# Sparse attention in a Trainium2 transformer kernel: value projections moved behind the queries, softmax factors one step later, values of an older pair before the turning of a younger one

## The chip, the cores and the metric

The kernel runs on one core of one Trainium2 chip. The metric is the device time of one execution in microseconds (us), lower is better.

## The reference

Two transformer blocks over 256 tokens of width 1024, in float32. The change touches one part of the second block, a sparse attention with three branches (compressed blocks, selected blocks, window) of 16 query heads in 4 groups:

```
kv = h @ w_kv                    # k_raw v_raw k_sel v_sel k_win v_win, 4 groups x 64
k_cmp, v_cmp = silu(blocks(k_raw) @ w1) @ w2, silu(blocks(v_raw) @ w1) @ w2
qg = h2 @ w_qg                   # 1024 query columns, 48 gate columns
gates = sigmoid(qg[..., 1024:])
p_c = softmax(q @ k_cmp.T + bias) * has_any
p_s = softmax(q @ k_sel.T + bias); p_w = softmax(q @ k_win.T + bias)
o = g0 * (p_c @ v_cmp) + g1 * (p_s @ v_sel) + g2 * (p_w @ v_win)
x = x + o @ w_o
```

With 256 tokens all selected blocks are taken, so the selected and the window branch see the same causal keys. `blocks` makes 15 overlapping blocks of 32 tokens.

## The kernel before

All is written by hand, engine by engine, each with its own in-order list of instructions; semaphores are waited for with `wait_ge`. SyncE loads the weights in chunks of 128 x 2048 into a ring of three slots (`raw`). For each chunk ScalarE writes a rounded high half (L385, `w_hi`), VectorE the rest (L724, `w_lo`, "a split"), and TensorE makes three products per tile of weights (high x high, high x low, low x high: L1362 to L1364, and L1425 to L1427 where tokens come out on partitions). Only when TensorE is through with chunk c (`chunk_used`) may the halves of chunk c + 3 be written: `nxt(c)` in ScalarE's and VectorE's lists.

Around the change the order is, before:

- TensorE: `kv_raw` 0 and 1, `k_att` 0 and 1, two transposes of the norm factor, `v_att` 0 and 1, query 0, the gates (48 products with 48 columns, L1425 to L1427), the first matrix of the compression (`phi`, four chunks, 96 products, L1782 to L1784), scores of pair 0 (L1711), query 1, query 2, small products of the compression, scores of pair 1, query 3, scores of the compressed branch (L1821, 32 records with 14 or 30 columns).
- VectorE: scaled raw values (L1175), 16 additions that lay out the blocks (L1185), splits, the low parts of the operand (L763), keys (L1194), values (L1201), low parts of the blocks (L741), query (L1210), gates, then the pair work.

Then a loop over eight pairs of heads. Step t issues, on TensorE, the scores of pair t (`n_score`), the turning (transposes) of the probabilities of pair t - 2 (`n_turn`, L1734 to L1739, banks 5 to 7), and the values of pair t - 3 (`n_out`, L1755 to L1763). On VectorE: `n_tops` adds the bias and takes the maximum of four parts per head in one custom instruction each (L1251), then a small instruction negates the maxima (L1254); `n_copies` copies turned probabilities out of PSUM (L1271, L1273); `n_factors` (L1262, L1264) waits for all eight exponentials of its pair. On ScalarE: `n_exps` (eight exponentials with sums, L673) and copies (L682, L684). On GpSimd two passes per pair multiply the probabilities by the factors (L288). In step 2 VectorE also does the softmax of the compressed branch (L1327 to L1334), in step 3 TensorE transposes it, and it is copied (L703, L1337). Scores of the next pair need the maxima of the last one, since the banks 2 to 4 are the only ones for scores.

Of the kernel before, what the change touches and what calls it, by code (L numbers as in the profile page):

```python
# [22 lines left out]
P = 128  # L23
# [23 lines left out]
          ("kv_raw", 2), ("k_att", 2), ("v_att", 2), ("nsa_q0", 1), ("nsa_gate", 1), ("phi", 4), ("nsa_q", 3),  # L47
# [8 lines left out]
NSA_Q_BANK = (6, 7, 6, 0)  # L56
PHI_BANK = (5, 0)
# [79 lines left out]
def program(nc, x_t, p_t, positions, weights, small, consts, rel_bias, bias_rows, bias_skew, out):  # L137
    with ExitStack() as ctx:
# [16 lines left out]
        nsa_p = nc.alloc_sbuf_tensor_at("nsa_p", [P, 4, S], F32, offset=x_at + 2 * 2 * 768 * 4)  # L155
        over = nc.sbuf_base
        gate_or_bias = sb("gate_or_bias", [P, 16, S])
        heads = sb("heads", [P, 16, S])
        x_f, y_f = sb("x_f", [P, KT, S]), sb("y_f", [P, KT, S])
        y_hl = sb("y_hl", [P, KT, 2, S], F32R)  # L160
# [4 lines left out]
        y_h, y_l = y_hl[:, :, 0, :], y_hl[:, :, 1, :]  # L165
        sq = sb("sq", [P, KT, S])
# [52 lines left out]
        n_near, n_ptx = sem("n_near"), sem("n_ptx")  # L219
# [10 lines left out]
        def cst(name, n, i=0):  # L230
# [29 lines left out]
        n_own = [flat(t_ab), nsa_p[:, 0:2, :].rearrange("p a b -> p (a b)"),  # L260
                 nsa_p[:, 2:4, :].rearrange("p a b -> p (a b)")]
# [56 lines left out]
        def _(pool):  # L318
# [49 lines left out]

            pool.wait_ge(op_lo, PC["blk_v"] + 1)
# [9 lines left out]
        def _(act):  # L379
# [269 lines left out]
            act.wait_ge(g_raw, 1)  # L649
            nc.scalar.activation(nsa_g[:, :, :], nsa_g[:, :, :], ACT.Sigmoid).then_inc(g_sig, 1)  # L650
            nxt(C["nsa_gate"])
            nxt(C["phi"])

# [13 lines left out]
            def n_exps(k):  # L667
# [3 lines left out]
                for m, ap in enumerate(n_parts(k)):  # L671
                    q, e, b = 1 - m // 2, k % 2, m % 2
                    nc.scalar.activation(ap, ap, ACT.Exp, bias=ns[:, 1, q, e, b:b + 1],  # L673
                                         accum_out=ns[:, 2, q, e, b:b + 1]).then_inc(n_exp, 1)
# [42 lines left out]
        def _(dve):  # L717
# [452 lines left out]
            for w in range(2):  # L1170

                dve.wait_ge(chunk_used, C["kv_raw"] + w + 1)
                if w == 1:
                    dve.wait_ge(blk_ready, 4)
# [833 lines left out]
```

## Time and profile before

| | |
|---|---|
| time of three runs, median (lowest to highest) | 1287.74 us (1286.16 to 1290.9) |
| the profiled execution: time, span | 1289.02 us, 1287.0 us |
| mean granted TensorE clock | 0.976 of 2.4 GHz |
| busy: TensorE, VectorE, ScalarE, GpSimd | 1233.5, 892.9, 647.1, 231.2 us |
| chain that ended last | TensorE 86%, VectorE 8%, ScalarE 4%, issue 2% |
| the sparse attention up to its output projection | 909.0 to 1073.3 us |

Times in the rows are microseconds from the start of the span. A row's bracket says how long the engine had been idle before it and what ended that. "PEclk" is the granted TensorE clock as a share of 2.4 GHz.

### The profile page before, as it was taken

The numbers are of one execution on the slowest core, as the hardware profiler recorded it, in microseconds if no ns is written. First come the engines' busy times: TensorE is split into PE (matmuls) and PEld (weight loads), VectorE is DVE, ScalarE is ACT, GpSimd is POOL, SyncE is SP. The second block draws the span as 40 slices with busy tenths as digits, with TensorE's granted clock in tenths as the row PEclk, the third lists the DMA queues.
The fourth block names the chain that finished last, engine by engine and source line by source line (L and its number), as shares of the span: only waits on it lengthen the run. The fifth ranks groups of instructions, "written<-read, shape, count | busy, mean of one in ns | idle before, by whom it ended". The sixth has DMA issues, their size and how long they took to land.

```text
span 1287.0 us, 19911 instructions
## 1 busy us (share of the span) xinstructions
PE 1233.5 (96%) x7952; PEld 1094.7 (85%) x7952; DVE 892.9 (69%) x1241; ACT 647.1 (50%) x851; POOL 231.2 (18%) x114
## 2 busy tenths in 40 slices
PE   5999999999999999999999999999999579999996
PEld 4888889977789888888999988888999448888885
DVE  6877667786867787766887776655767574766554
ACT  6655545541664665545633655444535454555441
POOL 1444200002000244400000045300001230355000
PEclk9999999998999999999999999999989799999998
DMA  6655554461635465555445455555555011455540
GB/s 260 212 183 192 197 196 171 157 229 32 166 107 173 159 218 182 189 194 197 164 164 196 166 205 189 194 197 194 199 197 197 33 34 66 166 194 197 196 164 33
DMA packets 31042, 217.35 MB, mean 169 GB/s; under 512 B 3408, under 2 KB 3584, under 8 KB 5488
## 3 DMA queue, kind: packets, MB, share of 16 engines
q1 hardware_dynamic: 29616, 210.66, 46.4%
q0 software_dynamic: 1344, 5.53, 1.7%
q8 instruction: 60, 0.98, 0.3%
q14 instruction: 22, 0.18, 0.0%
HBM read 215.10 MB, written 4.22 MB: 170 GB/s over the span
## 4 chain that ended last, share of the span: by engine, by line
PE 86%; DVE 8%; ACT 4%; issue 2%; DMA 0%; DVEq 0%; SPq 0%; ACTq 0%
PE bank L1369 37%; PE bank L1370 18%; PE bank L1362 7%; PE bank L1364 7%; PE bank L1363 7%; DVE w_hl L724 2%; ACT w_hl L385 1%; PE bank L1425 1%; PE bank L1426 1%; PE bank L1427 1%; DVE y_f L1185 1%; ACT x_f L673 1%; PE bank L1552 1%; PE bank L1711 1%; PE bank L1821 1%
## 5 line engine op out<-in xcount | busy, mean ns | idle before, releaser
L724 DVE TENSOR_TENSOR w_hl<-raw,w_hl 128x2048 fp32r<-128x2048 f32 x197 | 452.0, 2296 | 121.6 <-ACT w_hl L385 120.7
L385 ACT ACTIVATE w_hl<-raw 128x2048 fp32r<-128x2048 f32 x197 | 375.1, 1907 | 133.6 <-PE bank L1364 60.3
L1369 PE MATMUL bank<-x_hl,w_hl 128*128 128x512 f32 x864 | 303.1, 397 | 12.6 <-DVE w_hl L899 12.6
L1369 PE MATMUL bank<-hidden,w_hl 128*128 128x512 f32 x864 | 299.7, 394 | 0.0
L335 POOL TENSOR_TENSOR hidden<-hid_f,hidden 128x256 fp32r<-128x256 f32 (+1 forms) x76 | 189.4, 2492 | 529.1 <-ACT hidden L472 309.6
L1370 PE MATMUL bank<-x_hl,w_hl 128*128 128x256 f32 x864 | 240.6, 278 | 0.0
L1370 PE MATMUL bank<-hidden,w_hl 128*128 128x256 f32 x864 | 239.3, 277 | 0.0
L1369 PEld LDWEIGHTS bank<-x_hl,w_hl 128*128 128x128 f32 x864 | 163.3, 189 | 50.6 <-issue 12.5
L1369 PEld LDWEIGHTS bank<-hidden,w_hl 128*128 128x128 f32 x864 | 162.0, 188 | 37.6
L1362 PE MATMUL bank<-x_hl,w_hl 128*128 128x256 f32 x576 | 166.8, 290 | 1.0 <-DVE x_hl L741 0.6
L1363 PE MATMUL bank<-x_hl,w_hl 128*128 128x256 f32 x576 | 164.7, 286 | 0.0
L1364 PE MATMUL bank<-x_hl,w_hl 128*128 128x256 f32 x576 | 164.7, 286 | 0.0
L1370 PEld LDWEIGHTS bank<-x_hl,w_hl 128*128 128x128 f32 x864 | 163.5, 189 | 0.1
L1370 PEld LDWEIGHTS bank<-hidden,w_hl 128*128 128x128 f32 x864 | 162.2, 188 | 0.0
L451 ACT ACTIVATE second<-bank 128x512 f32<-128x512 f32 (+1 forms) x108 | 57.6, 533 | 199.2 <-PE bank L1370 199.2
L1369 PE MATMUL bank<-y_hl,w_hl 128*128 128x512 f32 x352 | 122.4, 394 | 0.0
L1362 PEld LDWEIGHTS bank<-x_hl,w_hl 128*128 128x128 f32 x576 | 112.2, 195 | 4.9 <-issue 2.6
L1363 PEld LDWEIGHTS bank<-x_hl,w_hl 128*128 128x128 f32 x576 | 112.4, 195 | 0.1
L1364 PEld LDWEIGHTS bank<-x_hl,w_hl 128*128 128x128 f32 x576 | 112.3, 195 | 0.0
L816 DVE TENSOR_TENSOR t_ab<-bank,second 128x512 f32<-128x512 f32 x76 | 52.6, 691 | 76.8 <-ACT second L451 58.6
L1362 PE MATMUL bank<-y_hl,w_hl 128*128 128x256 f32 (+1 forms) x352 | 100.3, 285 | 0.6 <-DVE w_hl L724 0.6
L1363 PE MATMUL bank<-y_hl,w_hl 128*128 128x256 f32 (+1 forms) x352 | 99.5, 283 | 0.0
(305 smaller groups left out, 1650.3 us busy)
## 6 DMA issues: line engine op xcount, KB each, us to landing
raw<-weights SPq DMA_DIRECT2D x198, 1024.0 KB, 4.9
bias_skew<-bias_rows POOLq DMA_DIRECT2D x1, 3072.0 KB, 23.6
gate_or_bias<-bias_skew POOLq DMA_DIRECT2D x1, 2048.0 KB, 10.7
h<-x_t SPq DMA_DIRECT2D x1, 1024.0 KB, 4.9
out_t<-x_f SPq DMA_DIRECT2D x4, 256.0 KB, 2.1
con<-consts SPq DMA_DIRECT2D x1, 672.5 KB, 12.2
heads<-p_t POOLq DMA_DIRECT2D x1, 256.0 KB, 3.1
par<-small SPq DMA_DIRECT2D x1, 199.5 KB, 4.9
```

Source lines behind the costliest of these rows:

```text
L335: nc.gpsimd.tensor_tensor(hidden[:, at, 1, :], src, hidden[:, at, 0, :].bitcast(F32), ALU.subtract).then_inc(hid_lo, 1)
L385: nc.scalar.activation(w_hi[:, s, :], raw[:, s, :], ACT.Copy).then_inc(hi_split, 1)
L451: nc.scalar.activation(dst, src, ACT.Copy).then_inc(second_out, 1)
L673: nc.scalar.activation(ap, ap, ACT.Exp, bias=ns[:, 1, q, e, b:b + 1], accum_out=ns[:, 2, q, e, b:b + 1]).then_inc(n_exp, 1)
L724: V.tensor_tensor(w_lo[:, s, :], raw[:, s, :], w_hi[:, s, :].bitcast(F32), ALU.subtract).then_inc(lo_split, 1)
L816: V.tensor_tensor(t_ab[:, :, :], bank[:, s:s + 2, 0:S], second[:, j % 2, :, :], ALU.add).then_inc(ab_ready, 1)
L1185: ins = V.tensor_tensor(dst[:, :, 2 * t + e, :], src[:, :, t, half:half + NCMP], pe[rows, :].rearrange("p (l n) -> p l n", n=1).to_broadca ...
L1362: mm(out_, w_hi[:, s, c:c + m], x[:, 0, :], start=start, stop=False, **kw)
L1363: mm(out_, w_hi[:, s, c:c + m], x[:, 1, :], start=False, stop=False, **kw)
L1364: return mm(out_, w_lo[:, s, c:c + m], x[:, 0, :], start=False, stop=stop, **kw)
L1369: mm(out_, w_hi[:, s, c:c + m], x, start=start, stop=False, **kw)
L1370: return mm(out_[:, 0:S], w_lo[:, s, c:c + m], x[:, 0, :], start=False, stop=stop, **kw)
```

## The change

The value projections leave their place behind the keys: chunk order, and order on all engines, put them behind the queries, one before the scores of the compressed branch and one behind scores 1. ScalarE evicts them (`v_in`) instead of VectorE. The gates are computed with features on partitions (24 products of 256 columns, weights padded to 128 columns) and turned by two transposes. The block layout goes to tiles of its own (`blk_h`, `blk_l`), with the second half of it behind the keys. Queries 1 to 3 come before any score. The softmax of the compressed branch stands before the loop, its transposes in step 2. `n_tops` gives the negated sum and its minimum, so that the negation goes; `n_exps` uses scale -1. In the loop VectorE makes the factors of pair t - 1 behind the maxima of pair t, and TensorE does the values of pair t - 3 ahead of the turning of pair t - 2.

```diff
-          ("kv_raw", 2), ("k_att", 2), ("v_att", 2), ("nsa_q0", 1), ("nsa_gate", 1), ("phi", 4), ("nsa_q", 3),
+          ("kv_raw", 2), ("k_att", 2), ("nsa_q0", 1), ("nsa_gate", 1), ("phi", 4), ("nsa_q", 3), ("v_att", 2),
...
-NSA_Q_BANK = (6, 7, 6, 0)
-PHI_BANK = (5, 0)
+NSA_Q_BANK = (3, 6, 7, 5)
+PHI_BANK = (1, 4)
...
# ScalarE
-            for j in range(1, 6):
-                nxt(c + j)
-            hi(x_hf[:, 0:960], y_flat[:, 0:960], blk_ready, 4, C["nsa_q0"])
-            hi(x_hf[:, 960:1920], y_flat[:, 960:1920], blk_ready, 8)
+            nxt(c + 1)
+            for j in range(2):
+                nxt(C["k_att"] + j)
+            hi(blk_h[:, 0, 0:960], y_flat[:, 0:960], blk_ready, 4)
             nxt(C["nsa_q0"])
...
+            hi(blk_h[:, 1, 0:960], y_flat[:, 960:1920], blk_ready, 8)
             nxt(C["nsa_gate"])
             nxt(C["phi"])
+            act.wait_ge(g_tr, 1)
+            nc.scalar.activation(nsa_g[:, :, :], bank[:, 5, 0:96].rearrange("p (a b) -> p a b", a=2),
+                                 ACT.Sigmoid).then_inc(g_sig, 1)
...
+            def v_in(w):
+
+                act.wait_ge(chunk_used, C["v_att"] + w + 1)
+                for t in range(2):
+                    nc.scalar.activation((n_vs, n_vw)[w][:, t, :], bank[:, 6 + w, t * 256:t * 256 + 256], ACT.Copy,
+                                         scale=r_tok[:, 0, t:t + 1]).then_inc(v_done, 1)
+
+            for j in range(1, 4):
+                nxt(NSA_Q[j])
             n_exps(0)
             n_exps(1)
-            nxt(NSA_Q[1])
-            n_exps(2)
-            n_exps(3)
-            nxt(NSA_Q[2])
+            v_in(0)
             for q in range(2):
                 c = c_p[:, q, :, :, 0:c_n[q]]
                 act.wait_ge(c_sub, q + 1)
                 nc.scalar.activation(c, c, ACT.Exp).then_inc(c_exp, 1)
+            n_exps(2)
+            n_exps(3)
+            nxt(C["v_att"])
+            v_in(1)
...
-                if t == 3:
+                if t == 2:
                     act.wait_ge(c_pt, 1)
                     nc.scalar.activation(c_t[:, 512:1024], bank[:, 1, :], ACT.Copy).then_inc(c_ptc, 1)
-                    nxt(NSA_Q[3])
+                if t == 4:
+                    nxt(C["v_att"] + 1)
...
# VectorE
+            for w in range(2):
+                raw_in(w)
                 nxt(C["kv_raw"] + w)
                 for j in range(2 * w, 2 * w + 2):
                     operand_piece("mix1", y_h, y_l, j)
             for w in range(2):
+                keys_in(w)
                 nxt(C["k_att"] + w)
+                blocks(0, (w,))
             dve.wait_ge(rt_mm, 2)
             st.done(V.tensor_copy(r_tok[:, 0, :], bank[:, SUMS, 0:256:128]))
...
+            lo(blk_l[:, 0, 0:960], y_flat[:, 0:960], blk_h[:, 0, 0:960])
+            blocks(1, (0, 1))
...
+            V.tensor_tensor(t_a[0:48, :], bank[0:48, 2, 0:S], r_sb[0:48, :], ALU.mult).then_inc(g_raw, 1)
             nxt(C["nsa_gate"])
+            lo(blk_l[:, 1, 0:960], y_flat[:, 960:1920], blk_h[:, 1, 0:960])
+            nxt(C["phi"])
...
-                    st.inc(V.tensor_tensor_reduce(dst, src, bias if m < 2 else bias[:, 128:256], 1.0, -3e38,
-                                                  ALU.add, ALU.max, ns[:, 0, 1 - m // 2, e, m % 2:m % 2 + 1]))
-                st.wait()
-                V.tensor_scalar(ns[:, 1, :, e, :], ns[:, 0, :, e, :], -1.0, None, ALU.mult).then_inc(n_max, 1)
+                    ins = V.tensor_tensor_reduce(dst, src, bias if m < 2 else bias[:, 128:256], -1.0, 3e38,
+                                                 ALU.add, ALU.min, ns[:, 1, 1 - m // 2, e, m % 2:m % 2 + 1])
+                ins.then_inc(n_max, 1)
...
             for t in range(2, PAIRS + 2):
                 if t < PAIRS:
                     n_tops(2 * t)
                     n_tops(2 * t + 1)
+                if t - 1 < PAIRS:
+                    n_factors(t - 1)
                 n_copies(t - 2)
-                if t < PAIRS:
-                    n_factors(t)
...
+                if t == 4:
+                    nxt(C["v_att"] + 1)
...
# TensorE
             query(0)
-            pe.wait_ge(kv_done, 5)
-            arrived(C["nsa_gate"] + 1)
-            tokens(C["nsa_gate"] % RING, lambda t: bank[:, 7, t * 48:t * 48 + 48], 48, range(KT), y_hl, 0,
-                   True, True).then_inc(chunk_used, 1)
...
+            c = C["nsa_gate"]
+            arrived(c + 1)
+            for k in range(KT):
+                last = product(bank[:, 2, 0:S], c % RING, k * P, P, y_hl[:, k, :, :], k == 0, k == KT - 1)
+            last.then_inc(chunk_used, 1)
...
+                if w == 0:
+                    pe.wait_ge(g_raw, 1)
+                    for t in range(2):
+                        ins = T(bank[:, 5, 48 * t:48 * t + 48], t_a[0:48, P * t:P * t + P],
+                                con[0:48, CN["ident"]:CN["ident"] + 48])
+                    ins.then_inc(g_tr, 1)
             query(1)
...
-            n_score(1)
+            pe.wait_ge(g_sig, 1)
             query(3)
-
+            pe.wait_ge(q_done, 1)
+            n_score(0)
...
+            pe.wait_ge(q_done, 3)
+            value(0)
             pe.wait_ge(q_done, 4)
             pe.wait_ge(cmp_done, 2)
...
             ins.then_inc(c_scores, 1)
+            n_score(1)
+            value(1)
 
             for t in range(2, PAIRS + 3):
                 if t < PAIRS:
                     n_score(t)
+                if t == 3:
+                    pe.wait_ge(c_ptc, 2)
+                if t >= 3:
+                    n_out(t - 3)
+                if t == 2:
+                    pe.wait_ge(v_done, 4)
                 if t - 2 < PAIRS:
                     n_turn(t - 2)
-                if t == 3:
+                if t == 2:
...
-                    pe.wait_ge(c_ptc, 2)
-                if t >= 3:
-                    n_out(t - 3)
```

## Rows read from the trace of the kernel before

**Rows 1.** Busy time by stretch: us, each engine busy (instructions), PEclk, DMA share, GB/s

```profile
909.00:1073.30 164.30, 140.09 (x1059) 122.40 (x1057) 108.62 (x266) 79.33 (x183) 27.35 (x18) 0.88 0.35 122
909.00:932.80 23.80, 23.80 (x198) 23.54 (x196) 19.86 (x33) 14.00 (x19) 1.20 (x1) 1.00 0.63 222
932.80:975.70 42.90, 40.41 (x289) 40.24 (x289) 29.74 (x30) 18.68 (x13) 0.95 (x1) 0.84 0.56 195
975.70:1009.70 34.00, 29.21 (x238) 27.64 (x237) 18.17 (x55) 14.42 (x37) 7.83 (x4) 0.87 0.44 157
1009.70:1073.30 63.60, 46.67 (x338) 30.98 (x337) 40.85 (x150) 32.23 (x115) 17.37 (x12) 0.85 0.05 18
```

**Rows 2.** Waits, 909 to 1073.3: who waited for whom, total, times, longest

```profile
PE bank L1755 <- DVE y_f L1337: 5.8, 1, 5.8
...
PE bank L1821 <- DVE heads L1210: 4.8, 1, 4.8
PE bank L1734 <- ACT nsa_t L684: 4.7, 3, 1.8
...
PE bank L1425 <- DVE w_hl L724: 2.5, 1, 2.5
```

**Rows 3.** Busy time by stretch: four at the lower clock, one not

```profile
936.40:939.80 3.40, 3.40 (x19) 3.40 (x18) 3.40 (x5) 0.00 (x0) 0.00 (x0) 0.52 0.88 306
956.80:966.90 10.10, 10.10 (x49) 10.10 (x49) 4.41 (x4) 2.88 (x3) 0.00 (x0) 0.50 0.35 117
1002.70:1014.70 12.00, 11.97 (x54) 10.90 (x55) 4.17 (x20) 1.31 (x5) 2.35 (x2) 0.50 0.26 87
1028.80:1035.10 6.30, 6.28 (x30) 3.65 (x32) 3.24 (x1) 1.21 (x1) 2.33 (x2) 0.50 0.15 25
...
1035.50:1062.30 26.80, 19.33 (x166) 12.76 (x164) 20.01 (x85) 16.30 (x64) 8.68 (x6) 1.00 0.08 32
```

**Rows 4.** Groups by line and shape, 909 to 1073.3: busy us, mean ns

```profile
L724 DVE TENSOR_TENSOR w_hl<-raw,w_hl 128x2048 fp32r<-128x2048 f32 x16 | 38.0, 2372 | 15.0 <-ACT w_hl L385 14.9
L385 ACT ACTIVATE w_hl<-raw 128x2048 fp32r<-128x2048 f32 x16 | 30.5, 1908 | 24.5 <-PE bank L1427 12.1 <-PE bank L1364 9.1 <-PE bank L1784 3.2
...
L1185 DVE TENSOR_TENSOR y_f<-t_ab,par 64x240 f32<-64x240 f32 x16 | 8.8, 572 | 0.3
...
L1271 DVE COPY nsa_t<-bank 128x512 f32<-128x512 f32 x8 | 5.5, 690 | 3.5 <-PE bank L1739 3.5
...
L763 DVE SCALAR_TENSOR_TENSOR y_hl<-h,par,y_hl 128x256 fp32r<-128x256 f32 x8 | 3.3, 479 | 0.0
```

**Rows 5.** The chain that ended last: start, us, what

```profile
1002.73 7.03 PE bank L1821 x32
```

**Rows 6.** Busy time by stretch: one step's scores, turning, values

```profile
1045.92:1047.42 1.50, 1.50 (x12) 1.08 (x13) 1.15 (x2) 1.50 (x8) 0.00 (x0) 1.00 0.00 0
1047.42:1048.92 1.50, 1.50 (x16) 1.33 (x14) 0.19 (x1) 1.50 (x8) 0.00 (x0) 1.00 0.05 11
1048.92:1051.13 2.21, 2.21 (x21) 1.05 (x20) 2.06 (x12) 0.26 (x1) 1.92 (x2) 1.00 0.00 0
```

**Rows 7.** Instructions in order of time, one step of the pair loop

```profile
1042.64 1.90 POOL L288 TENSOR_TENSOR x_f<-x_f,stat 128x1024 f32<-128x1024 f32 x1
1042.76 1.81 DVE L1254 TENSOR_SCALAR stat<-stat 128x4 f32<-128x4 f32 x1
...
1044.60 0.51 ACT L673 ACTIVATE second<-second,stat 128x256 f32<-128x256 f32 x1 [2.99 <-DVE stat L1254]
...
1048.73 0.20 DVE L1262 RECIPROCAL stat<-stat 128x8 f32<-128x8 f32 x1 [1.66 <-ACT nsa_p L673]
...
1050.21 1.90 POOL L288 TENSOR_TENSOR second<-second,stat 128x1024 f32<-128x1024 f32 x1
```

**Rows 8.** Instructions in order of time, VectorE: softmax of the compressed branch

```profile
1019.89 1.86 DVE L1334 TENSOR_TENSOR y_f<-y_f,mv 128x112 f32<-128x112 f32 x1
...
1021.88 0.41 DVE L1334 TENSOR_TENSOR y_f<-y_f,mv 128x240 f32<-128x240 f32 x1
```

More of the change, by code:

```diff
@@ L1169, in _, with raw_in, blocks @@
             dve.wait_ge(r_ready, 2)
-            for w in range(2):
+            kv_f = (t_ab, hid_f)
+            def raw_in(w):
                 dve.wait_ge(chunk_used, C["kv_raw"] + w + 1)
-                if w == 1:
-                    dve.wait_ge(blk_ready, 4)
-                V.tensor_tensor(t_ab[:, :, :], two(bank[:, TURN + w, :]), r_two, ALU.mult).then_inc(kv_done, 1)
+                V.tensor_tensor(kv_f[w][:, :, :], two(bank[:, TURN + w, :]), r_two, ALU.mult).then_inc(kv_done, 1)
+            def blocks(w, halves):
                 dve.wait_ge(kv_done, w + 1)
                 pe = col("pe_k" if w == 0 else "pe_v", 0, 16)
-                for half in range(2):
+                for half in halves:
                     for e in range(2):
                         rows = slice(64 * half, 64 * half + 64)
-                        src = t_ab[64 * e:64 * e + 64, :, :].rearrange("p a (n l) -> p l a n", l=16)
+                        src = kv_f[w][64 * e:64 * e + 64, :, :].rearrange("p a (n l) -> p l a n", l=16)
                         dst = y_flat[rows, 960 * w:960 * w + 960].rearrange("p (l g n) -> p l g n", l=16, g=4)
@@ L1188, in _, with keys_in @@
                         ins.then_inc(blk_ready, 1)
+            def keys_in(w):
+                dve.wait_ge(chunk_used, C["k_att"] + w + 1)
+                V.tensor_tensor((n_ks, n_kw)[w], two(bank[:, (6, 0)[w], :]), r_two, ALU.mult).then_inc(kv_done, 1)
+            for w in range(2):
+                raw_in(w)
                 nxt(C["kv_raw"] + w)
@@ L1290, in _ @@
                 rows = slice(32 * g, 32 * g + NCMP)
-                ins = V.tensor_copy(v_cmp[rows, :], bank[rows, 1, 320:384])
+                ins = V.tensor_copy(v_cmp[rows, :], bank[rows, 0, 320:384])
             ins.then_inc(cmp_done, 1)
-            query(2)
-            n_tops(2)
-            n_tops(3)
             nxt(NSA_Q[2])
-            n_factors(1)
             query(3)
+            n_tops(0)
+            n_tops(1)
+            nxt(NSA_Q[3])
+            n_factors(0)
             c_max, c_sum, c_rec, c_fac = (c_stat[:, m, :, :] for m in range(4))
@@ L1689, in _ @@
             transposed_factors(2, r_sb)
-            for w in range(2):
-                c = C["v_att"] + w
-                arrived(c + 1)
-                tokens(c % RING, lambda t: bank[:, 1 + w, t * 256:t * 256 + 256], 256, range(KT), x_hl, 0, True,
-                       True).then_inc(chunk_used, 1)
             T = nc.tensor.transpose
@@ L1944, in pack_weights @@
     mlp(w["mlp_w1_2"][0], w["mlp_w2_2"][0])
-    for k in (0, 1, 2, 4, 3, 5):
-        add(rows(w["w_kv_2"][:, 256 * k:256 * k + 256]))
+    kv = lambda k: rows(w["w_kv_2"][:, 256 * k:256 * k + 256])
+    for k in (0, 1, 2, 4):
+        add(kv(k))
     qg = w["b_w_qg_2"][0]
@@ L1953, in pack_weights @@
     pairs(q[:, 256:])
+    for k in (3, 5):
+        add(kv(k))
     pairs(w["b_w_o_2"][0].reshape(16, 64, D)[NSA_ORDER].reshape(D, D))
```

101 lines of the change are left out of this document (45 added, 56 removed).

## The prediction

> **What bounds it now.** I read the page's chain first: TensorE carries 86% of it, so time is saved only where TensorE waits or runs slowly. Then the busy time by stretch. The change lies between 909.0 us (first key/value projection) and 1073.3 us (output projection of the sparse attention): 164.3 us in which TensorE is busy for 140.1 and idle for 24.2, at a mean granted clock of 0.88 [rows 1]. The view of waits says for whom it idles [rows 2]: 5.8 us before the first value products (L1755) for VectorE's copy of the compressed probabilities, 4.8 before the compressed scores (L1821), 4.7 in the pair loop before the turning (L1734), 2.5 where the first value projection waits for its low half. Last the clock [rows 3]: four stretches, 31.8 us together, lie at about 0.50, 1.2 GHz instead of 2.4, so they hold 15.9 us of loss; small ones elsewhere make it about 17. Three of them follow the three long waits; ahead of the fourth (956.8) TensorE had not waited but begun, at 954.2, the products with 48 columns (L1425 to L1427 with y_hl). The stage at full clock without a wait would be 140.1 - 17 = 123 us. What can be won is waits and clock, 41 us, and a little work.
>
> In steady state the pair loop is no TensorE loop. Scores, turning and values take 1.5, 1.5 and 2.2 us, 5.2 in all [rows 6], but a step takes 7.57 (GpSimd's long passes start at 1042.64 and 1050.21). The ring is VectorE to ScalarE and back [rows 7]: four maxima (1.2 us, from 1041.5), then the 4-element negation L1254, which takes 1.81 beside GpSimd's pass, which ends at 1044.54; only then do the exponentials start (1044.60); VectorE, in order, waits for all eight in the factors (1048.73) before it takes the next maxima.
>
> **What changes, with prices.**
>
> *Value projections later.* Same 96 products (2 x 5.8 us). TensorE goes on with query 0 at 932.8, whose low half is there at 926.3, so the 2.5 us wait goes. But VectorE is the next late one. From 918.6 it does, before the second phi chunk has its low half: five splits at 2.25, 16 block adds at 0.57, eight gained pieces at 0.41, five scaled evictions at about 0.65 (as the copy L1271 of the same form), one 960-column low part at 1.1 (half a split's 2048 columns) [rows 4]: 11.3 + 9.1 + 3.3 + 3.3 + 1.1 = 28.1, and about 1.9 of waits for ScalarE's high halves (1.9 each): ready at 948.6. TensorE gets there at 932.8 + 5.8 (query 0) + 2.9 (gates) + 2.9 (first phi chunk) = 944.4. A new wait of 4.4 us. The next, for blk_v's low part (948.7 + 0.4 + 2.25 + 1.1 = 952.5 against 952.1), is 0.4.
>
> *Gates as 24 products of 256 columns* instead of 48 with 48 columns, and two small transposes: at 0.12 a product (198 in 23.8 us before 932.8 [rows 1]) 2.9 + 0.4 us, against 5.4 at full clock (0.112 each); at 0.50 it was 7.8 (954.2 to 961.95). So 2.1 less work. They are also no longer the stretch in which the clock fell (the 10.1 us of [rows 3]).
>
> *Queries before all scores.* Phi 2.9 + 5.8, query 1 to 964, query 2 with transposes and small products to 971.4, query 3 to 977.2, scores 0 to 978.7. ScalarE and VectorE have the halves of these chunks by then (958.3, 960.6, 964.6). *Values as cover.* Value 0 (5.8) stands before the compressed scores, scores 1 and value 1 (5.8) behind them. The 4.8 us wait at L1821 is gone, since query 3 is scaled at 977.9 and the scores start at 984.5; the wait behind them for the compressed softmax (part of the 5.8) lies under value 1. The 32 small products took 7.0 us at 0.50 [rows 5]; at the upper level half, 3.5; both ends are kept, 3.5 taken. Value 1 ends at 995.3, scores 2 at 996.8.
>
> *The softmax of the compressed part* goes from inside step 2 to before the loop: about 3.7 us of VectorE (the two rows of L1334, 2.3, and 1.4 of small ones ahead of them), ending by about 996, under value 1. L1334 took 1.86 on 112 elements while GpSimd was at work, and 0.41 on 240 elements after it [rows 8]. I keep the long price in the sum; the short one changes nothing, because value 1 covers both.
> The Trainium skill (SBUF — State Buffer, "Who interferes with whom") says that a VectorE instruction with two SBUF inputs and a GpSimd one that reads SBUF exclude each other for a whole instruction, the first to start winning. Row 8's pair and the 1.81 of [rows 7] agree in length. Applied to what now stands in the loop it speaks against the change: the weight split at t = 4 has two SBUF inputs, and if GpSimd's two passes of pair 3 are under way it waits up to 1.9 longer, or they wait 2.3 for it and the turning after them; the forecast by it would be 1275.
>
> *Maxima with sign turned, no negation*: 16 instructions of L1254 go, 1.8 us at worst on the ring [rows 7]. The same custom instruction with minimum in place of maximum isn't in this trace: from nothing extra to twice its time (1.2 us for four); I take nothing, since it streams the same elements. ScalarE's scale of -1 is an operand, likewise nothing.
>
> *Factors one step later.* VectorE's step is maxima 2.3, factors 0.45, copies 0.69 or 1.4, low parts 0.3 on average: 4 us. ScalarE's is eight exponentials and a copy, 4.1 (1044.60 to 1048.73), every other time a second copy, and high parts of 0.3 on average: 4.4 to 4.9. TensorE's is 5.2 and becomes the bound. GpSimd's two passes, 1.9 and about 1, end before the turning that needs them, which stands last in the step. *Values first, turning second* gives the copies of a pair 1.5 us of cover (the scores), as against 3 before; on even pairs ScalarE's copy of bank 7 comes 0.7 to 2 us late.
>
> Following the queues from 996.8 on, waits of TensorE: 1.0 for ScalarE's copy of the second values, 1.2 for the maxima behind a weight split, 2.5 for the transposed probabilities (both engines have a step's work in front), 0.7, then 2.7 where at t = 4 VectorE stands for the high and low half of chunk v_att+1+3 (1.9 + 2.3) before maxima 10, then 1.3, 3.2, 1.3, 0.7 and 1.3 in the last steps, where copies come late. That is 15.9 less overlaps, 14.8. The work is 8 x 1.5 + 5 x 1.5 + 8 x 2.2 + 1.0 = 38.1. So the output projection would start near 996.8 + 38 + 15 = 1050 at full clock; with handoffs of 0.1 that I left out, 1051 to 1052.
>
> *The clock* is not given by this. After the wait of 4.4 us I expect a low stretch as after the 2.5 us one (3.4 us [rows 3]) to twice that, 2.5 us of loss; behind the small score products one of 1 to 2; in and after steps 3 and 6 together some 2 to 3. I take 6.5 (13 us at the lower level instead of some 34). Start of the projection: 1058.6, gain 14.7 us.
>
> **Sum.** The profiled execution took 1289.0 (span 1287.0). Less 14.7: 1274.3. The runs' median is 1.3 below it, 1287.7; forecast **1273.0**. Behind 1073.3 nothing changes, and the weights for it are split in time (chunk nsa_out at 984).
>
> **Rivals.**
> (a) Forecast, 0.60: 1264 to 1280.
> (b) The clock stays up nearly everywhere, loss under 2 us, and TensorE's loop runs at 5.3 a step: gain 20 to 22, so 1266 to 1268, and 1262 if half of the late waits go too. For it: the loop had 1.00 from 1035.5 to 1062.3 with TensorE busy for 19.3 of 26.8 us [rows 3]. Against: the new 4.4 us wait. 0.14, beside the part in (a).
> (c) The lower level lasts as long as before (34 us, loss 17), since waits of 1 to 3 us stand in every step: gain 41 + 2.1 - 19.6 - 17 = 6.5, 1281. For it: the waits of 2.5, 4.8 and 5.8 us each had a low stretch with them [rows 2, 3]; against: the 7.5 us of waits between 1035.5 and 1062.3 had none. 0.18.
> (d) Other side: the loop runs at the lower level throughout, and TensorE, now its bound, sets the step. At half the clock 5.2 becomes up to 10.4 a step, against 7.57. Work of 38 becomes 76, from 997 to 1073 and some 5 of waits, after 5 lost earlier: 1083, ten later: 1298. It decides as soon as some 44 us of the stage are at the lower level. 0.04.
> (e) The reordering changes nothing measurable, because the ring VectorE-ScalarE stays at 7.5 (something else blocks VectorE) and the early part gives back its wait: 1285. Against: L1254 and the in-order wait both leave the ring. 0.04.
>
> Measurement can tell about 0.5%, 6.4 us (runs spread from 1286.2 to 1290.9). Faster by more: all of (a) and (b), half of (c): 0.83; within: half of (c), (e): 0.12; slower: (d) and a remainder, 0.05. Range for 8 in 10: 1262 to 1283.
>
> **What would show it.** The output projection starting near 1058 (1050 to 1066) instead of 1073.3; idle time of the stage near 20 instead of 24, one wait of 4 to 5 us at the second phi chunk for L724; no PE wait at the compressed scores; steps of GpSimd's passes 5.3 to 6 apart instead of 7.57; no 1.8 us small VectorE instruction ahead of the exponentials; low stretches of 10 to 16 us in sum. It would be wrong if the custom instruction with minimum is slower, if the clock lies low in the loop, or if copies of bank 7 hold the values so long that steps stay above 7.

## The result, and the profile after

Changed, the kernel takes **1271.6 us** (median of 4 runs, 1270.5 to 1275.5) against 1289.3 before (4 runs, 1286.2 to 1291.2): ratio 0.9878, 95% interval [0.9856, 0.9899]. The profiled execution has a span of 1268.6 us against 1287.0.

Busy time by stretch in the changed kernel (columns as in [rows 1]): the whole stage, the two stretches at the lower clock, and the pair loop from the scores of pair 3 on.

```profile
911.40:1054.70 143.30, 124.83 (x1037) 109.32 (x1035) 97.05 (x245) 81.01 (x187) 25.65 (x20) 0.98 0.39 140
951.00:954.50 3.50, 3.13 (x15) 3.14 (x16) 3.50 (x4) 3.32 (x3) 0.00 (x0) 0.51 0.57 173
992.00:995.50 3.50, 3.50 (x17) 2.52 (x16) 2.98 (x13) 0.70 (x2) 0.00 (x0) 0.51 0.02 5
...
1005.84:1054.67 48.83, 35.79 (x304) 23.78 (x304) 25.81 (x111) 30.53 (x109) 20.25 (x14) 1.00 0.11 40
```

The stage is 143.3 us long instead of 164.3 [rows 1], 21.0 less. It begins 2.4 us later, though every instruction before it is the same; so 18.4 us of the span are saved. TensorE is busy for 124.8 instead of 140.1 and idle for 18.5 instead of 24.2; the mean clock is 0.98 instead of 0.88. Two stretches at 1.2 GHz, 7 us together, stand where there were four with 31.8 [rows 3] and a fifth that those rows leave out (1062.5 to 1066.0, at 0.51). Most of what was won is clock.

The view of waits for the same stretch, as [rows 2]:

```profile
PE bank L1723 <- DVE stat L1272: 4.8, 3, 2.5
PE bank L1795 <- DVE w_hl L742: 4.2, 1, 4.2
PE bank L1767 <- ACT nsa_t L691: 3.1, 2, 2.2
PE bank L1767 <- DVE nsa_t L1293: 2.9, 2, 1.5
PE bank L1767 <- ACT y_f L720: 2.4, 1, 2.4
PE bank L1767 <- DVE nsa_t L1291: 0.9, 1, 0.9
```

L1723 are the scores, L1795 the first product of a phi triple, L1767 the first of a pair's value products, L1272 the maxima, L691 ScalarE's copy of bank 7, L1291 and L1293 VectorE's copies. Gone are the waits at the compressed scores (4.8), at the first value projection (2.5) and the 5.8 at the first value products, of which 2.4 are left. New is one at the second phi chunk. The places that answer to [rows 5 and 8] and to the copies, in order of time (rows with "x32" and "x12" are from the view of the chain, the others from the view of instructions):

```profile
951.37 0.57 PE L1795 MATMUL bank<-w_hl,blk_h 128*120 128x256 f32 x1 [4.20 <-DVE w_hl L742]
...
988.36 3.49 PE bank L1847 x32
991.86 2.73 PE bank L1723 x12
...
998.14 0.28 DVE L1342 TENSOR_TENSOR y_f<-y_f,mv 128x112 f32<-128x112 f32 x1
...
998.55 0.41 DVE L1342 TENSOR_TENSOR y_f<-y_f,mv 128x240 f32<-128x240 f32 x1
...
1021.07 0.65 PE L1767 MATMUL bank<-nsa_t,heads 128*64 128x256 f32 x4 [0.87 <-ACT nsa_t L691]
```

The 32 small products take 3.49 us in the chain (7.03 before [rows 5]) and nothing waits ahead of them. They run at the upper level; the stretch from 992.0 on begins right behind them, in the scores of pair 1 (2.73 us there, 1.5 at full clock). The compressed softmax no longer meets GpSimd: 0.28 and 0.41 us instead of 1.86 and 0.41 [rows 8].

GpSimd, in order of time, for five pairs in a row (the first pass of each pair):

```profile
1017.76 1.04 POOL L290 TENSOR_TENSOR t_ab<-t_ab,stat 128x512 f32<-128x512 f32 x1 [4.72 <-DVE stat L1284]
...
1027.67 1.04 POOL L290 TENSOR_TENSOR hid_f<-hid_f,stat 128x512 f32<-128x512 f32 x1 [7.01 <-DVE stat L1284]
...
1034.11 1.04 POOL L290 TENSOR_TENSOR nsa_p<-nsa_p,stat 128x512 f32<-128x512 f32 x1 [3.54 <-DVE stat L1284]
...
1038.08 1.04 POOL L290 TENSOR_TENSOR t_ab<-t_ab,stat 128x512 f32<-128x512 f32 x1 [1.08 <-DVE stat L1284]
...
1044.59 1.04 POOL L290 TENSOR_TENSOR hid_f<-hid_f,stat 128x512 f32<-128x512 f32 x1 [3.62 <-DVE stat L1284]
```

The distances are uneven: 9.9, 6.4, 4.0 and 6.5 us. The last three steps (1027.67 to 1044.59) have a mean of 5.64; in the kernel before, the same three (1041.65 to 1064.34) have 7.56 each, the step of [rows 7]. Over the six steps from pair 1 to pair 7 it is 6.40 against 10.37, where the steps before also hold the compressed softmax.

### The profile page after: what moved, and what is told of

The parts are those of the page before. It is cut to its first block, busy times and chain, and to the rows that moved or that the text cites. A ratio compares the mean times of both kernels' runs of the same rounds, so it can differ in the third digit from the quotient of the medians.

```text
span 1268.6 us, 19851 instructions
## 1 busy us (share of the span) xinstructions
PE 1218.6 (96%) x7930; PEld 1081.7 (85%) x7930; DVE 881.4 (69%) x1220; ACT 648.9 (51%) x855; POOL 229.5 (18%) x116
## 4 chain that ended last, share of the span: by engine, by line
PE 87%; DVE 7%; ACT 4%; issue 2%; DMA 0%; DVEq 0%; SPq 0%; ACTq 0%
PE bank L1386 38%; PE bank L1387 19%; PE bank L1379 7%; PE bank L1380 7%; PE bank L1381 7%; DVE w_hl L742 2%; ACT w_hl L390 1%; PE bank L1564 1%; PE bank L1442 1%; DVE y_f L1206 1%; PE bank L1444 1%; PE bank L1443 1%; PE bank L1723 0%; PE bank L1450 0%; ACT x_f L680 0%
## 5 line engine op out<-in xcount | busy, mean ns | idle before, releaser
L742 DVE TENSOR_TENSOR w_hl<-raw,w_hl 128x2048 fp32r<-128x2048 f32 x197 | 450.7, 2289 | 118.3 <-ACT w_hl L390 117.5
L1381 PE MATMUL bank<-x_hl,w_hl 128*128 128x256 f32 x576 | 164.3, 285 | 0.0
L1380 PE MATMUL bank<-x_hl,w_hl 128*128 128x256 f32 x576 | 164.3, 285 | 0.0
L1379 PE MATMUL bank<-y_hl,w_hl 128*128 128x256 f32 (+1 forms) x360 | 102.5, 285 | 0.6 <-DVE w_hl L742 0.6
L1380 PE MATMUL bank<-y_hl,w_hl 128*128 128x256 f32 (+1 forms) x360 | 101.8, 283 | 0.0
## 6 DMA issues: line engine op xcount, KB each, us to landing
gate_or_bias<-bias_skew POOLq DMA_DIRECT2D x1, 2048.0 KB, 10.9
```

The source lines that it names most:

```text
L742: V.tensor_tensor(w_lo[:, s, :], raw[:, s, :], w_hi[:, s, :].bitcast(F32), ALU.subtract).then_inc(lo_split, 1)
L1379: mm(out_, w_hi[:, s, c:c + m], x[:, 0, :], start=start, stop=False, **kw)
L1380: mm(out_, w_hi[:, s, c:c + m], x[:, 1, :], start=False, stop=False, **kw)
L1381: return mm(out_, w_lo[:, s, c:c + m], x[:, 0, :], start=False, stop=stop, **kw)
```

## The experiments

To compare the runs, each stage is measured in its own profile from the product of the sum of squares (914.75 us before, 917.28 changed) to the end of the last values, and cut at the scores of pair 3 (1015.41 before, 1005.84 changed): ahead of the cut lie projections, phi layers, small products and compressed scores, behind it the steady loop. "Idle" is TensorE's idle time in the stage; "clock" is the sum over slices of 0.5 us of what the granted clock lacks to 1.00 (a stretch at the lower level counts about half its length, also where TensorE waits). Each row of the last five columns is one profile. Ratios are to the kernel before on the same chip.

| run | median us | ratio [95%] | ahead | behind | stage | idle | clock |
|---|---|---|---|---|---|---|---|
| before | 1289.3 | 1 | 100.7 | 57.9 | 158.6 | 24.2 | 20.5 |
| changed | 1271.6 | 0.9878 [0.9856, 0.9899] | 88.6 | 48.9 | 137.5 | 18.4 | 3.4 |
| change_again | 1270.3 | 0.9870 [0.9838, 0.9903] | 88.5 | 48.9 | 137.5 | 18.4 | 3.4 |
| factors_same_step | 1277.7 | 0.9936 [0.9916, 0.9956] | 90.7 | 53.2 | 143.9 | 18.7 | 11.9 |
| negation_back | 1276.2 | 0.9918 [0.9888, 0.9949] | 89.9 | 53.9 | 143.9 | 19.0 | 10.2 |
| old_ring | 1276.9 | 0.9936 [0.9912, 0.9960] | 90.6 | 57.8 | 148.4 | 20.9 | 13.6 |
| loop_only | 1282.0 | 0.9957 [0.9938, 0.9976] | 98.2 | 52.4 | 150.6 | 19.1 | 15.4 |
| gates_48 | 1273.2 | 0.9896 [0.9863, 0.9928] | 87.2 | 52.0 | 139.1 | 12.2 | 10.2 |
| values_early | 1270.7 | 0.9886 [0.9851, 0.9921] | 89.4 | 48.1 | 137.5 | 19.4 | 3.4 |
| values_and_gates_back | 1273.2 | 0.9902 [0.9873, 0.9931] | 90.3 | 52.0 | 142.3 | 15.8 | 10.2 |
| turning_first | 1267.5 | 0.9849 [0.9820, 0.9878] | 89.3 | 47.5 | 136.8 | 16.2 | 6.8 |
| split_after_loop | 1271.6 | 0.9883 [0.9863, 0.9903] | 89.3 | 46.8 | 136.1 | 15.7 | 5.4 |
| both_splits_late | 1260.6 | 0.9798 [0.9778, 0.9818] | 87.2 | 42.4 | 129.6 | 9.7 | 5.1 |
| copies_first | 1260.5 | 0.9781 [0.9758, 0.9804] | 87.0 | 39.6 | 126.5 | 8.6 | 3.4 |

The stage begins between 913.3 and 919.1 us in these profiles although nothing before it differs between the changed versions. The stage is therefore the finer measure, and a difference of 3 us between two medians is no proof alone. But each stage is one execution, with the clock that this one had.

With the low clock counted only while TensorE is busy (17.7 us before, 3.2 changed), stage less idle time less clock is 116.6 us before and 115.8 changed, and 115.0 to 116.7 in every run: the work is nearly the same everywhere. Of the 21.1 us, then, some 14.5 are clock, 5.8 idle time and 0.8 work.

**The ring: factors and negation.** Undone one at a time, then both. The exponential's scale of -1 goes with the negation; all else stays changed, the values first too.

```
 # factors_same_step                     # negation_back (and both: old_ring)
-    if t - 1 < PAIRS:                   -  tensor_tensor_reduce(..., -1.0, 3e38, ALU.add, ALU.min, ns[:, 1, ...])
-        n_factors(t - 1)                +  tensor_tensor_reduce(..., 1.0, -3e38, ALU.add, ALU.max, ns[:, 0, ...])
     n_copies(t - 2)                     +  st.wait()
+    if t < PAIRS:                       +  tensor_scalar(ns[:, 1, :, e, :], ns[:, 0, :, e, :], -1.0, None, ALU.mult)
+        n_factors(t)
```

> The changed kernel, but the factors of pair t stand again in step t behind the copies (those of pair 1 ahead of the loop). Theory A (the ring of VectorE and ScalarE set the loop): with no negation in it the ring is 1.2 us of maxima, 4.1 of exponentials and a copy, 0.45 of factors, so 5.9 to 6.3 us a step instead of about 5.3 to 6: the stage (143.3 us from the first key/value product to the output projection in the changed kernel) grows by 3 to 5 us, the time to 1274.5 to 1277. Theory B (the loop's edits are worth nothing, the gain is from the value projections as cover and the clock): stage and time unchanged within 1 us.

> The changed kernel, but with maxima and the small negation as before. Theory A: GpSimd's passes now start behind the maxima of the following step and are over before the next ones, so the negation takes its 0.17 us, 0.4 a step on VectorE, which is not the bound: stage +0 to +2 us. Theory B (the blocked negation alone, 1.8 us at worst a step, was what the loop lost before, wherever the factors stand): negations of 1 to 1.8 us again and stage +6 to +9 us.

> The changed kernel with both: factors in the same step and the negation back. Theory A: the ring of before is whole again, the negation waits for GpSimd's long pass (1 to 1.8 us a step), steps of 7.3 to 7.6 us, stage +9 to +12, time 1281 to 1284; more than the sum of the two single edits. Theory B: the loop's order is not the cause, no more than +2 us.

Either one undone costs 6.4 us of the stage, 4.3 and 5.0 behind the cut. For the factors that is more than the 3 to 5 expected. For the negation it is the size of theory B with the short negations of theory A, so neither holds as written. Both undone cost 10.9, within the 9 to 12 expected, but less than the two single edits together (12.8), and the median is 1276.9 instead of 1281 to 1284. Behind the cut the stage is as long as before, 57.8 against 57.9, from different parts: TensorE idle for 13.4 instead of 16.7 us, and 10.2 instead of 6.8 us lost to the clock. GpSimd's long passes and the negations that meet them in old_ring:

```profile
1035.90 1.89 POOL L290 TENSOR_TENSOR second<-second,stat 128x1024 f32<-128x1024 f32 x1
...
1043.47 1.89 POOL L290 TENSOR_TENSOR x_f<-x_f,stat 128x1024 f32<-128x1024 f32 x1
...
1051.03 1.89 POOL L290 TENSOR_TENSOR x_f<-x_f,stat 128x1024 f32<-128x1024 f32 x1
```

```profile
1036.73 1.09 DVE L1275 TENSOR_SCALAR stat<-stat 128x4 f32<-128x4 f32 x1
...
1038.96 0.17 DVE L1275 TENSOR_SCALAR stat<-stat 128x4 f32<-128x4 f32 x1
...
1043.57 1.81 DVE L1275 TENSOR_SCALAR stat<-stat 128x4 f32<-128x4 f32 x1
```

The passes are 7.57 and 7.56 us apart, the ring of [rows 7] to the hundredth, and the negation that starts beside one ends with it (1043.57 + 1.81 = 1045.38; the pass 1045.36). GpSimd itself is a part of this ring: in [rows 7] the long pass ends at 1044.54, the exponentials run from 1044.60 to 1048.7, the factors follow until 1049.2, then GpSimd's short pass (1.0 us), and at 1050.21 the next long one. That adds up to the 7.57, however long the negation is, since it ends with the pass.

With negation_back alone it took 0.17 us but for two of 0.29 and 0.42: the factors one step later keep GpSimd's passes away from it, and the last three steps are 5.60 us on average, as short as the changed kernel's 5.64. With factors_same_step the last two are 6.60 and 6.16. So the later factors alone take this ring away in the late steps, and the missing negation alone shortens it; only with both undone are there 7.56 again. Of the 6.4 us of either run only 0.3 and 0.6 are idle time; the rest shows as clock. How much of that the edit causes is not shown, since the clock moves between kernels for other reasons too (last section).

**Values first against turning first.** Only the order of two calls in a step of TensorE:

```
-                if t >= 3:
-                    n_out(t - 3)
 ...
                 if t - 2 < PAIRS:
                     n_turn(t - 2)
 ...
+                if t >= 3:
+                    n_out(t - 3)
```

> The changed kernel, but in a step TensorE turns the younger pair first and does the values of the older one second, as before. Theory A: copies get 3.7 us of cover instead of 1.6, the waits of the value products for copies (7 us in the stage) mostly go, and the turning waits some tenths a step for GpSimd: stage -3 to +2 us. Theory B (values first is part of the gain, since turning early waits for GpSimd's 3 us behind late factors): 1 to 2 us a step, stage +5 to +8.

The stage is 0.7 us shorter than changed, idle 2.2 less, clock 3.4 more. Its view of waits:

```profile
PE bank L1746 <- POOL x_f L290: 4.2, 3, 2.0
PE bank L1795 <- DVE w_hl L742: 4.2, 1, 4.2
PE bank L1723 <- DVE stat L1272: 4.0, 2, 2.6
PE bank L1746 <- ACT nsa_t L691: 2.9, 2, 2.0
```

The waits at the values (L1767, 9.3 us in the changed kernel) are all gone, and others of 7.1 stand at the turning (L1746): values first didn't help, and it hurts a little at most. Of the 4.0 us between the two profiled executions (1266.5 and 1270.5) 3.3 are an earlier start of the stage (913.98 against 917.28), ahead of which no instruction differs.

**The same kernel again.**

> The changed kernel once more, with a profile of its own. If the clock's falls belong to the places in the program, the stretches at the lower level stand at the same instructions as in the first profile (about 951 to 954.5 and 992 to 995.5 us, 3.4 us lost). If they are spread by chance among the steps that wait, they stand elsewhere, with 3 to 10 us lost, and differences of that size between other variants' clocks say nothing alone. Time 0.986 to 0.990 of the kernel before on this chip, as measured; idle time of TensorE in the stage again 18 to 19 us.

The low stretches stand at 950.5 to 954.5 and 991.5 to 995.5 again, at the same instructions, and the stage agrees to 0.1 us. So these two executions fell at the same places. It isn't so for every execution: the four runs of turning_first, one program, have mean granted clocks from 0.985 to 0.993 and times from 1268.8 to 1263.2 us.

**The loop's edits alone**, on the kernel before (the three loop edits of the diff; projections, gates and compressed softmax as before).

> The kernel before with the three edits of the loop alone (the negation folded into the maximum, factors one step later, values of the older pair ahead of the turning); the value projections stay behind the keys and the gates stay narrow. If the loop's edits are what opens the ring: the steps shrink from 7.57 to 5.5 to 6 us and the time is 8 to 11 us under before, 1276 to 1279 us. If they work only because the later value projections and queries gave the loop its material earlier (the product of moving things), the steps stay above 7 us and the gain is under 4 us.

The stage is 8.0 us shorter than before, 5.5 of them behind the cut: between the two cases. The last three steps of GpSimd's passes are 5.92 us on average, as expected, but the median is 1282.0 instead of 1276 to 1279. Waits and busy time by stretch:

```profile
PE bank L1819 <- DVE heads L1210: 4.3, 1, 4.3
PE bank L1753 <- ACT y_f L703: 3.9, 1, 3.9
```

```profile
999.50:1013.50 14.00, 13.01 (x58) 11.61 (x60) 6.01 (x27) 2.55 (x11) 0.38 (x1) 0.51 0.20 75
1023.50:1030.50 7.00, 7.00 (x36) 3.65 (x32) 4.05 (x12) 1.44 (x4) 0.00 (x0) 0.51 0.38 126
```

Idle time is nearly that of the changed kernel (19.1 against 18.4); what is missing is clock, 15.4 against 3.4. A long low stretch begins in or just behind each of the two waits that the early part of the change removes or halves, at the small products (996.2 to 1000.5) and at the compressed probabilities (1018.8 to 1022.7). The two halves of the change: early part alone (old_ring, which also keeps the values first) 10.2 us of the stage, loop alone 8.0, together 21.1. The 2.9 by which the whole is more than the sum are no larger than what the clock alone can differ by between two kernels.

**Gates and values put back.**

```
 # gates_48: 48 products of 48 columns, no turning after them
-            for k in range(KT):
-                last = product(bank[:, 2, 0:S], c % RING, k * P, P, y_hl[:, k, :, :], k == 0, k == KT - 1)
+            tokens(c % RING, lambda t: bank[:, 2, t * 48:t * 48 + 48], 48, range(KT), y_hl, 0, True, True)
 # values_early: chunks of v_att behind k_att again, evicted by VectorE into banks 1 and 2 before the blocks
-            value(0)   # before the compressed scores
-            value(1)   # behind the scores of pair 1
+            for w in range(2): tokens(..., lambda t: bank[:, 1 + w, t * 256:t * 256 + 256], 256, range(KT), x_hl, ...)
```

> Gates by 48 products of 48 columns, as in the kernel before, and no turning of them afterwards. The prediction's account: 48 products with 48 columns issue in about 2.1 us more than 24 with 256, and the clock falls beside them (before: 956.5 to 967 us at the lower level), so stage 2 to 5 us longer than the changed kernel's, 1273 to 1277 us. Rival: the clock falls only where TensorE waits, so the width of the products costs their issue time alone, under 2.5 us and with no stretch at the lower level beside the gates.

> The changed kernel with the value projections put back behind the keys, their eviction on VectorE, and the old order of the chunks; all else as changed. By the prediction's account value 1 no longer covers the compressed softmax, so 3 to 5 us of TensorE's wait come back at the compressed probabilities, and the early products fill the wait for the second phi chunk (4.2 us less there): net 0 to 4 us slower than changed, 1272 to 1276 us. If the place of the values is what made most of the gain, 6 to 10 us slower, 1278 to 1282 us.

> The changed kernel with two parts undone at once: the value projections behind the keys as in the run values_early, and the gates by 48 products of 48 columns as in gates_48. The loop and the order of the work around the phi layers, the small products and the compressed softmax stay changed. Stage of changed 137.5 us; values early alone 137.5, narrow gates alone 139.1, the loop's edits on the kernel before 150.6. If the parts add up: 139 to 140 us, idle 19 to 20, 3 to 7 us lost to the clock, 1272 to 1274 us; what is left to 150.6 then belongs to the new order around the phi layers, the small products and the compressed softmax. If narrow gates and the early values together bring the low clock back (no wait ahead of the gates that covers them): 143 us or more, with over 10 us lost to the clock, 1276 us or more.

*gates_48*: the wait for the second phi chunk is gone, since the longer gate products fill it, and the part ahead of the cut is 1.4 us shorter, not longer. The stage is 1.6 us longer, under the 2 to 5 expected, and its clock loss is 6.8 higher:

```profile
945.50:953.00 7.50, 7.50 (x40) 7.50 (x40) 7.35 (x12) 3.67 (x3) 0.00 (x0) 0.54 0.03 9
1010.50:1018.00 7.50, 7.50 (x42) 5.03 (x39) 1.29 (x2) 3.78 (x17) 2.89 (x2) 0.54 0.01 2
```

The first stretch stands at and after the narrow products, with no wait in it. It costs less than its 3.5 us of loss, as VectorE is late there anyway: the low half for the second phi chunk is ready at 953.04 and TensorE starts on it at 954.16.

```profile
950.76 2.28 DVE L741 TENSOR_TENSOR w_hl<-raw,w_hl 128x2048 fp32r<-128x2048 f32 x1
```

```profile
954.16 0.28 PE L1796 MATMUL bank<-w_hl,blk_h 128*120 128x256 f32 x1
```

Counted from the start of the stage that is 1.0 us later than in the changed kernel (35.05 against 34.09), and after it there is no low stretch like the one from 951.0 to 954.5. The second, in the loop, goes with a part behind the cut that is 3.1 us longer; that the narrow products are its cause is not shown. *values_early*: the stage is the same to 0.1 us. The early products fill the wait at phi (1.3 left of 4.2), and the compressed softmax, uncovered, gives it back as one wait of 5.7 before the scores of pair 2. With both put back the stage is 4.8 us longer, not 1.7: the parts don't add up. 1.7 lie ahead of the cut, where no wait at phi takes the longer gates any more, but where the clock also lost 1.7 us more, which no run tells apart; 3.1 lie behind it, as in gates_48. The 4.8 fall between the two expectations. But 8.3 us still lie between this kernel and loop_only. So most of the early part's gain belongs neither to the gates nor to the values' place, but to the rest of it, in which stand query 3 and its scaling ahead of the compressed scores, and the compressed softmax out of the loop. That rest was not taken apart.

**The splits in the loop, and a faster version.** The chain of work that ended last in the changed kernel runs through both splits that stand at and in the loop:

```profile
999.44 1.81 ACT w_hl L390
1001.27 2.29 DVE w_hl L742
...
1020.45 0.48 ACT nsa_t L691
1020.93 1.81 ACT w_hl L390
```

split_after_loop moves the one at t = 4 behind the loop. both_splits_late moves both and turns first. copies_first also reorders ScalarE, and moves VectorE's low halves of the output operands one step later (t in 6, 8, 9 instead of 5, 7, 9), so it tests both together:

```
                 n_copies(t - 2, 0)              # bank 5, was behind the exponentials of head pair 2t
                 if t < PAIRS:
                     n_exps(2 * t)
                 n_copies(t - 2, 1)              # bank 7, and at t = 2 the compressed copy
                 if t < PAIRS:
                     n_exps(2 * t + 1)
 ...
-            nxt(C["v_att"])                     # both engines: from before the loop
-                    nxt(C["v_att"] + 1)         # and from t = 4
+            nxt(C["v_att"])                     # behind the last high and low parts of y
+            nxt(C["v_att"] + 1)
```

> The changed kernel, with the split of the weight chunk at t = 4 (1.90 us on ScalarE, 2.29 on VectorE, which waits for it) put behind the loop on both engines; everything else as changed. If this split is what makes the wait of 2.55 us before the scores of pair 6, that wait goes and the stage (137.5 us from the sum of squares to the last values) falls by 2.5 to 4 us, time 1266.5 to 1268 against 1270.5. Rival: the chunk's transfer comes too late behind the loop, and TensorE waits for the third chunk of the last projection by 2 us or more, so the time stays within 1 us of changed.

> Turning ahead of the values as in the kernel before, all else as changed, and both splits of the loop (at its head and at t = 4) behind the loop. If the two splits hold VectorE and with it the scores (waits of 1.42 and 2.58 us in the run with turning first), the stage falls from 136.8 to 131 to 134 us, time 1260 to 1264 against 1267.5. Rival: two chunks late are more than the transfers catch up behind the loop, TensorE waits there 2 to 5 us, and the time is 1265 to 1269.

> The kernel with both splits late and turning first, and within a step ScalarE copies bank 5 ahead of the exponentials of the same step, bank 7 between them, the compressed copy with it, and VectorE's two low halves of the output operands one step later. If ScalarE's order makes the waits at the turning (2.02 us at the second pair, 0.91 at the fourth) these fall under 0.5 and the stage is 1.5 to 3 us shorter than with both splits late alone, 1258 to 1262 us. Rival: the copy ahead of the exponentials delays these, the rescaling on GpSimd comes later by as much, and the stage is the same or up to 2 us longer.

*split_after_loop*: the wait of 2.55 us goes and no wait comes behind the loop, but the stage falls by 1.4 only, under what was expected, and the time not measurably. Idle fell by 2.7, clock loss rose by 2.0, and another 1.4 are lost right behind the stage, in the rest of a low stretch from 1052.0 to 1055.5. *both_splits_late*: the stage falls by 7.3 against turning_first, 1.4 more than the most that was expected; no wait behind the loop, so the later transfers are covered. The waits for the maxima are gone. What is left there, and in copies_first:

```profile
PE bank L1793 <- DVE w_hl L741: 4.2, 1, 4.2
PE bank L1744 <- ACT nsa_t L691: 4.1, 3, 2.0
PE bank L1744 <- POOL x_f L290: 1.3, 2, 0.8
```

```profile
PE bank L1795 <- DVE w_hl L743: 4.2, 1, 4.2
PE bank L1746 <- POOL x_f L290: 3.7, 3, 1.7
PE bank L1746 <- POOL second L290: 0.5, 1, 0.5
```

With the copies first, the waits for ScalarE (4.1) become waits for GpSimd (1.3 before, 4.2 now), as the rival had it with its later exponentials; still the stage is 3.0 shorter, 1.7 by clock and 1.1 by idle time. The medians of the two don't tell them apart, as this stage happened to start 3.7 us later. Either beats the changed kernel by about 0.8 to 1.0% and the kernel before by 2.0 to 2.2%.

## Why the prediction was right

The forecast was 1273.0, measured 1271.6. The mechanism was right in its main steps: the two early waits go, one comes at the second phi chunk, the ring opens and the clock recovers. That the number fits so closely is partly luck. The stage gained 21.0 us, not 14.7, which is the size that rival (b) had (20 to 22); it also began 2.4 us later than before, which the forecast did not have, and the new clock loss was set too high. Step by step:

- **Work and waits ahead of the loop: right.** The new wait at the second phi chunk was put at 4.4 (the two times in the sum, 948.6 and 944.4, give 4.2) and is 4.20, for L742, the changed kernel's line of the split, as named. The further 0.4 for blk_v's low part didn't come. No wait at the compressed scores, small products 3.49 for 3.5, at the upper level as taken. The low stretch expected behind them came there (992.0 to 995.5).
- **Gates.** Priced as 2.1 us less work. True as work, worth little at this place: VectorE sets the time of the second phi chunk, and gates_48 starts it only 1.0 us later, with 3.5 us of low clock on the way. The sum had this in it (a wait of 4.4 behind the shorter gates), but the text does not say it. In all the wide form goes with a stage that is 1.6 us shorter; that this is clock is seen, that the gates cause it is not shown.
- **Values as cover.** Right that value 1 hides the compressed softmax, wrong that the move wins: values_early shows 0.
- **Minimum instead of maximum** cost nothing: L1272 takes 421 and 286 ns for 256 and 128 columns, L1251 had 418 and 284.
- **The ring opens: right**: the late steps are 7.56 with both edits undone and 5.64 with both. It was described as VectorE to ScalarE and back; GpSimd's two passes, 2.9 of the 7.57 us, are a part of it. **"TensorE's is 5.2 and becomes the bound": wrong.** Steps average 6.40 where 5.3 to 6 were to show it, and from the cut on TensorE is idle for 13.0 of 48.8 us. In the changed kernel the handoffs still bound the loop; close to TensorE's pace is only copies_first (39.6 us from the cut, of which 4.3 idle).
- **The loop's waits** were put at 14.8 (15.9 less overlaps). The row of waits from the loop's start is 1.1, 2.4, 0.9, 2.6, 1.1, 2.2, 1.5, 0.9, 1.5: 14.1. Foreseen were 1.0, 1.2, 2.5, 0.7, 2.7, 1.3, 3.2, 1.3, 0.7, 1.3; the 1.0 for the second values' copy didn't come, the one at t = 4 came as priced.
- **The clock** is the term that was mis-sized: 6.5 us of loss, measured 3.4. At phi 1.7 came for 2.5, behind the small products 1.7 for 1 to 2. It was also to fall "in and after steps 3 and 6", by 2 to 3, where it stayed at 1.00 through the whole loop from the cut on. Low stretches of 10 to 16 us in sum were to show the forecast; there are 7. The loss before was read as about 17; it is 17.7 while TensorE is busy and 20.5 with the waits. The 3.1 us less of loss are part of the 6.3 by which the stage beat the forecast (21.0 for 14.7). Another 2.3 is the loop at full clock: from the end of value 1 to the projection it takes 53.9 us (1000.82 to 1054.77), where the forecast had 56.2 (995.3 to some 1051.5), with a wait that didn't come and 1 to 2 us for handoffs that don't exist. The last 0.9 is spread over small terms. The 2.4 us later start of the stage took part of it back, so that the median came out within 1.4 us.
- **Rivals.** (b), the clock stays up nearly everywhere, has the size of the stage's gain and describes the loop's clock after, but not its steps of 5.3; and 3.4 us were lost to the clock, not under 2. (c), as long at the lower level as before, is what comes of half the change: loop_only and old_ring lose 15.4 and 13.6 us to the clock. (d) and (e) are out.
- **The rule of the Trainium skill** (SBUF — State Buffer, "Who interferes with whom"), by which the split at t = 4 could be held up, decided nothing here: the split took 2.29 us at 1022.76, while GpSimd was idle between 1020.65 and 1027.67. The rule holds where they meet: in factors_same_step the same split starts at 1027.24 beside a pass that ends at 1028.33, and takes 3.24.

```profile
1026.44 1.89 POOL L290 TENSOR_TENSOR x_f<-x_f,stat 128x1024 f32<-128x1024 f32 x1
```

```profile
1027.24 3.24 DVE L742 TENSOR_TENSOR w_hl<-raw,w_hl 128x2048 fp32r<-128x2048 f32 x1 [1.88 <-ACT w_hl L390]
```

That is 0.95 more than 2.29, about the 1.09 that were left of the pass. It was the overlap that the prediction feared; with the factors one step later it did not come. The negation of [rows 7] has one SBUF input, not two, so it is no case of the rule in the words that the prediction gives; that it waits for the pass is shown by the lengths alone.

## What to carry to other kernels

Where two engines hand to each other and a third runs beside them, write down the ring with all three in it and break it at every in-order wait: here either edit alone gave 4.5 of the 10.9 us of both, clock included. After that look in the chain of work for work that has no due time yet, as the two weight splits were: moving both out of the loop, with the old order of turning and values, gave another 0.8% on the 1.2% of the whole change. And when a stage mixes short waits with narrow products, judge an edit by idle time and granted clock together, since one fell while the other rose in gates_48, split_after_loop and turning_first.

## What the runs showed of the hardware

- **The clock isn't decided by the instructions at hand.** changed and split_after_loop have the same instructions until t = 4 of the loop. Behind the small products, in the scores of pair 1, changed runs at the lower level from 992.0 to 995.5 (0.51), split_after_loop doesn't, and gets a low stretch later, in the loop; at phi its low stretch is 7 us long, not 3.5. Busy time of split_after_loop by stretch, the second line from its small products over the scores of pair 1 to the first products of value 1:

```profile
949.50:956.50 7.00, 5.88 (x27) 5.56 (x27) 6.86 (x5) 4.07 (x3) 0.95 (x1) 0.51 0.70 248
991.30:995.50 4.20, 4.20 (x36) 3.74 (x36) 3.05 (x13) 0.71 (x2) 0.00 (x0) 1.00 0.11 45
1011.00:1014.50 3.50, 3.50 (x21) 2.64 (x18) 0.00 (x0) 0.79 (x4) 1.98 (x2) 0.52 0.00 0
```

  Two executions of changed had their low stretches at the same places, but the runs of turning_first differ in mean clock (0.985 to 0.993) without any edit. So 3 us of clock between two kernels, or more, can be the place at which a fall happened to come, and the last column of the table is not to be read finer than that.
- **A low clock needn't cost all its loss.** In gates_48 7.5 us at 0.54, a loss of 3.5, stood around a handoff that VectorE set, and TensorE reached it 1.1 us after the data were there. Before the change the clock was at 0.50 from 1025.0 to 1028.8 while TensorE waited, which costs it nothing; so the clock column of the table overstates the price by such waits (20.5 for 17.7).
- **The start of the stage moved by up to 5.8 us** (913.3 to 919.1) between kernels with the same instructions before it. Two profiles of the changed kernel agree in it to 0.1 us. Much of it is clock ahead of the stage: the loss from the start of the span, while TensorE is busy, is 1.7 us in old_ring (start 913.3), 5.1 before (914.8), 6.3 in changed (917.3) and 9.9 in copies_first (919.1). gates_48, with 4.8 and 919.1, does not fit that, and why the clock differs there stays open.
